# Depthwise convolution in two parts and row-by-row input split in the projection stage of a two-block hybrid model

## The reference

```python
def _grid_dwconv(u, w, grid_hw):
    b, t, ch = u.shape
    img = u.reshape(b, grid_hw[0], grid_hw[1], ch)
    out = lax.conv_general_dilated(img, w[:, :, None, :].astype(u.dtype), (1, 1), "SAME",
                                   dimension_numbers=("NHWC", "HWIO", "NHWC"),
                                   feature_group_count=ch)
    return out.reshape(b, t, ch)
```

## Time and profile before

| | us |
|---|---|
| three runs | 3732.07, 3729.84, 3727.48 |
| median | 3729.84 |
| the profiled execution, its time | 3728.76 |
| the profiled execution, its span | 3727.0 |
| PE busy in the span | 3390.9 |
| DVE busy | 1958.8 |
| ACT busy | 1435.2 |

### The profile page before, as it was taken

The page is one execution under the profiler, slowest core; times in us unless marked ns, Lnnn a source line. Parts: engine busy times, 40 slices in busy tenths (PEclk is TensorE's granted clock), DMA queues, the critical chain, the costliest instruction groups (busy, mean ns, idle before and its releaser), DMA issues.

```text
span 3727.0 us, 51106 instructions
## 1 busy us (share of the span) xinstructions
PE 3390.9 (91%) x20406; PEld 2828.4 (76%) x20406; DVE 1958.8 (53%) x2838; ACT 1435.2 (39%) x2196; POOL 218.7 (6%) x225
## 2 busy tenths in 40 slices
PE   1998776579999999999998999999999989999998
PEld 1776444457778877889855679999998557799998
DVE  6647577865534443446564544454446545444433
ACT  2532455344432333234345443343343444433322
POOL 1000033210000000000020000000000100000000
PEclk9999877569999999999999989999999989899999
DMA  5562101013333224223200002343432000023333
GB/s 194 182 201 93 51 15 59 10 55 113 108 118 117 90 94 164 94 88 121 81 1 29 24 24 83 106 140 92 136 113 76 1 29 24 30 86 109 113 94 100
DMA packets 94493, 321.82 MB, mean 86 GB/s; under 512 B 10352, under 2 KB 11632, under 8 KB 93488
## 3 DMA queue, kind: packets, MB, share of 16 engines
q1 hardware_dynamic: 76224, 249.66, 20.6%
q0 software_dynamic: 17312, 67.78, 5.2%
q10 hardware_dynamic: 720, 1.12, 0.1%
HBM read 295.38 MB, written 23.20 MB: 85 GB/s over the span
## 4 chain that ended last, share of the span: by engine, by line
PE 80%; DVE 12%; ACT 5%; DMA 1%; issue 1%; DVEq 0%; POOL 0%; ACTq 0%; SPq 0%; POOLq 0%
PE psum L146 76%; DVE mixer L171 4%; PE psum L149 3%; DVE mixer L181 2%; DVE wlo L171 1%; DVE arena L194 1%; DVE arena L171 1%; DVE junk L185 1%; ACT arena L155 1%; DVE mixer L198 1%; DVE region L171 1%; ACT whi L163 1%; ACT arena L163 0%; DMA stage<-in_wm 0%; ACT L155 0%
## 5 line engine op out<-in xcount | busy, mean ns | idle before, releaser
L146 PE MATMUL psum<-region,whi 128*128 128x260 f32 (+2 forms) x8896 | 1909.8, 312 | 22.8 <-DVE region L171 18.4
L146 PEld LDWEIGHTS psum<-region,whi 128*128 128x128 f32 (+1 forms) x8896 | 1444.1, 188 | 134.3 <-DVE region L171 16.8
L146 PE MATMUL psum<-region,wlo 128*128 128x260 f32 (+2 forms) x4448 | 1380.8, 310 | 0.0
L171 DVE TENSOR_TENSOR wlo<-stage,whi 128x1024 fp32r<-128x1024 f32 (+2 forms) x454 | 512.9, 1130 | 732.2 <-ACT whi L163 697.3
L146 PEld LDWEIGHTS psum<-region,wlo 128*128 128x128 f32 (+1 forms) x4448 | 839.7, 189 | 49.2
L163 ACT CAST whi<-stage 128x1024 fp32r<-128x1024 f32 (+2 forms) x454 | 441.7, 973 | 271.2 <-PE psum L146 177.7
L146 PE MATMUL psum<-arena 128*128 128x65 f32 (+8 forms) x2064 | 423.6, 356 | 2.8 <-ACT arena L155 1.2
L163 ACT COPY arena<-psum 128x512 f32<-128x512 f32 (+10 forms) x428 | 190.4, 445 | 416.3 <-PE psum L146 382.2
L146 PE MATMUL psum<-mixer 64*128 64x128 f32 (+6 forms) x1140 | 230.5, 446 | 121.0 <-DVE mixer L198 55.0
L146 PEld LDWEIGHTS psum<-arena 128*128 128x128 f32 (+4 forms) x2064 | 256.6, 181 | 100.3 <-issue 90.8
L154 ACT ACTIVATE arena<-psum 128x260 f32<-128x260 f32 (+1 forms) x236 | 101.0, 428 | 596.0 <-PE psum L146 595.6
(11 more groups left out here) (144 smaller groups left out, 2771.5 us busy)
## 6 DMA issues: line engine op xcount, KB each, us to landing
stage<-in_w SPq DMA_DIRECT2D x144, 512.0 KB, 3.5
stage<-in_wi SPq DMA_DIRECT2D x55, 512.0 KB, 4.2
stage<-in_wm SPq DMA_DIRECT2D x48, 512.0 KB, 3.4
stage<-in_wo SPq DMA_DIRECT2D x48, 512.0 KB, 3.5
stage<-in_wg SPq DMA_DIRECT2D x44, 512.0 KB, 3.3
stage<-in_wu SPq DMA_DIRECT2D x44, 512.0 KB, 3.3
stage<-in_wd SPq DMA_DIRECT2D x32, 512.0 KB, 3.3
arena<-xr_scratch POOLq DMA_DIRECT2D x7, 2080.0 KB, 8.8
```

The lines of the kernel that those rows point to most:

```text
L146: return Issued(self, self.e and self.e.matmul(out, w, x, start=start, stop=stop, skip_group_check=True))
L171: return Issued(self, e and e.tensor_tensor(out, a, b, op))
```

## The change

The convolution is cut in two by image rows. Part "a" makes output rows 0 to 6 (448 elements), which need image rows 0 to 7 only, and stands beside the half units of chunk 1 (ticks 11 to 22); its accumulators lie in a part of `vt` that chunk 2 fills later. Part "b" makes rows 7 to 15 (576 elements) in ticks 4 to 17 of chunk 2. The context's convolution moves to ticks 5 to 9 of chunk 1. The norm of chunk 1 starts at tick 2 of chunk 0 instead of tick 0. The wait on the whole chunk is gone: in the last half of a chunk, rows 2kk and 2kk+1 of the next chunk's input are split one tick after unit kk, when the product that used them has ended (`row_free`, `next_rows`). Six deferred rows move from chunk 1 to chunk 2.

```diff
-    CONV = [(m, part) for m in range(6) for part in range(3)] + [(m, 3) for m in range(5)]
+    ROWS_A, ROWS_B = (0, 7), (7, 16)
+    CONV_A = [(m, "a", part) for m in range(6) for part in range(3)]
+    CONV_B = [(m, "b", part) for m in range(6) for part in range(3)]
+    acc_a, acc_c = at(9000, 2, 448), at(9896, 2, 256)
 
     def proj_ticks(ch):
-        todo = [("norm", ch + 1, s) for s in NORM] if ch < 2 else [("conv", *c) for c in CONV]
-        heads = 6 if ch else 5
-        n = [0]
+        plan = [[] for n in range(11 + 12)]
+        if ch < 2:
+            for i, s in enumerate(NORM):
+                plan[i + (0 if ch else 2)].append(("norm", ch + 1, s))
+        if ch == 1:
+            for m in range(5):
+                plan[5 + m].append(("conv", m, "c", 0))
+            for i, c in enumerate(CONV_A):
+                plan[11 + i * 12 // len(CONV_A)].append(("conv", *c))
+        if ch == 2:
+            for i, c in enumerate(CONV_B):
+                plan[4 + i * 14 // len(CONV_B)].append(("conv", *c))
 
         def tick():
-            n[0] += 1
-            k = 1 if ch < 2 else 0 if n[0] <= heads else 2
-            out, todo[:k] = todo[:k], []
-            return out
-        return tick, todo
+            return plan.pop(0)
+        return tick
...
         if ch == 1:
-            return [19 + n] if n < 23 else []
-        return [42 + n] if n < 6 else []
+            return [19 + n] if n < 17 else []
+        return [36 + n] if n < 12 else []
...
+    def next_rows(ch, half, kk):
+
+        return (2 * kk, 2 * kk + 1) if ch < 2 and half == (2 if ch else 0) else ()
+
+    def row_free(ch, k):
+        return sproj.pe["unit", W.last["tok", ch - 1, 2 if ch > 1 else 0, k // 2]]
...
+        def act_row(ch, k):
+            N = chunks[ch][2]
+            if ch:
+                e.wait_ge(*row_free(ch, k))
+            e.wait_ge(*A["aff", ch, k])
+            e.copy(hh[:, k, 0:N], tmp[:, k, 0:N]).then_inc(*A.up("hi", ch, k))
         for ch, (src, s0, N, base) in enumerate(chunks):
-            tick, todo = proj_ticks(ch)
-            if ch:
-                e.wait_ge(*T["chunk", ch - 1])
-            for k in range(8):
-                e.wait_ge(*A["aff", ch, k])
-                e.copy(hh[:, k, 0:N], tmp[:, k, 0:N]).then_inc(*A.up("hi", ch, k))
+            tick = proj_ticks(ch)
+            for k in range(8 if ch == 0 else 0):
+                act_row(ch, k)
...
+                    for k in next_rows(ch, half, kk - 1) if kk else ():
+                        act_row(ch + 1, k)
+                for k in next_rows(ch, half, 3):
+                    act_row(ch + 1, k)
                 for t in range(N // 128):
                     ps = psum[:, bank.of["tok", ch, half, t], :]
...
                 for tap in range(part * 3, part * 3 + 3):
-                    v = img[:, tap // 3:tap // 3 + 16, tap % 3:tap % 3 + 64]
+                    v = img[:, r0 + tap // 3:r1 + tap // 3, tap % 3:tap % 3 + 64]
                     wc = P["convw"][:, m * 9 + tap:m * 9 + tap + 1]
                     if tap == 0:
-                        e.wait_ge(*A[("wi", 2, m), 0])
-                        e.wait_ge(*A["hi", 2, 7])
+                        e.wait_ge(*A[("wi", 1 if kind == "a" else 2, m), 0])
+                        if kind == "b":
+                            e.wait_ge(*A["hi", 2, 7])
```

More of the change, by code:

```diff
@@ L662, in dve_steps @@
             for m in (4, 5):
-                e.wait_ge(*sproj.act["conv", m])
+                e.wait_ge(*sproj.act["conv", m, "b"])
             e.wait_ge(*T["dt"])
@@ L815, in act_proj @@
                         ring += 1
-            for s in todo:
-                step(s)
         A.mark("end")
@@ L851, in step @@
                         e.scalar_tensor_tensor(acc, v, wc, acc, ALU.mult, ALU.add).then_inc(*D.up())
-                D.mark("conv", m, part)
+                D.mark("conv", m, kind, part)
                 return
@@ L876, in dve_proj, with dve_row @@
         dve_mod(e, beside)
-        for ch, (src, s0, N, base) in enumerate(chunks):
-            tick, todo = proj_ticks(ch)
-            if ch:
-                e.wait_ge(*T["chunk", ch - 1])
-            for k in range(8):
-                e.wait_ge(*A["hi", ch, k])
-                e.tensor_tensor(hl[:, k, 0:N], tmp[:, k, 0:N], hh[:, k, 0:N].bitcast(F32), ALU.subtract).then_inc(
-                    *D.up("lo", ch, k))
+        def dve_row(ch, k):
+            N = chunks[ch][2]
+            if ch:
+                e.wait_ge(*row_free(ch, k))
+            e.wait_ge(*A["hi", ch, k])
+            e.tensor_tensor(hl[:, k, 0:N], tmp[:, k, 0:N], hh[:, k, 0:N].bitcast(F32), ALU.subtract).then_inc(
+                *D.up("lo", ch, k))
+        for ch, (src, s0, N, base) in enumerate(chunks):
+            tick = proj_ticks(ch)
+            for k in range(8 if ch == 0 else 0):
+                dve_row(ch, k)
             for key in proj_gemms(ch):
@@ L894, in dve_proj @@
                     if (ch, half) == (2, 2):
-                        assert not todo
                         dve_steps(e, kk)
-            for s in todo:
-                step(s)
+                    for k in next_rows(ch, half, kk - 1) if kk else ():
+                        dve_row(ch + 1, k)
+                for k in next_rows(ch, half, 3):
+                    dve_row(ch + 1, k)
         D.mark("end")
```

44 lines of the change are left out of this document (23 added, 21 removed).

## The result

| | before | changed |
|---|---|---|
| median of 7 runs, us | 3729.84 | 3715.43 |
| lowest to highest | 3726.88 to 3732.21 | 3712.53 to 3719.31 |
| ratio, 95% interval | | 0.9963 [0.9952, 0.9975] |
| the profiled execution, its time | 3728.76 | 3715.06 |
| its span | 3727.0 | 3713.3 |

The change makes the kernel 14.4 us faster. The forecast was 33 us (3697), with 3690 to 3710 as its own range: the sign was right, the size wrong by more than half. The wide range reached to 3716 and just holds the result.

The account below looks back on a forecast made before the run. TensorE bounds the kernel (91% busy), but VectorE bounds chunk 2 with the convolution. Terms -28 - 6 + 7 - 6 = -33 us against 3728.76 give 3695.8, median 1.1 above: 3697 us, own range 3690 to 3710.

Parts of the forecast that it names:

- The wide range: Whole kernel: 3680 to 3716 us, taking in the bounds, the all-hidden case and half of the Silu rival.
- 1. Chunk 2's convolution work: Chunk 2 keeps nine rows of 64; 6 us of waits stand for the 34: -28 us, bounds -33 and -20.
- 2. The boundary between chunks 1 and 2: Rows split early, so the 4.25 us idle and slow first unit (1.5) go: -6 us, bounds -6 and -3.
- 3. Chunk 1 carries the other half: Chunk 1's steps 11 to 22 and context steps make units late: +7 us, bounds 2 and 16.
- 4. The boundary between chunks 0 and 1: Later norm and earlier rows mostly remove 2.82 us idle and 2.8 of the first unit: -6, bounds 0 and -10.
- 5. Extra taps: VectorE: 108 instructions for 54 on the same elements, 12.5 us more work, already counted in parts 1 and 3.
- the line: Tap time on VectorE interpolated between 0.50 us (256 elements) and 1.31 (1024): 0.70 on 448, 0.84 on 576.
- Every Silu costs its round: Rival: all 17 Silus leave VectorE idle 1.9 us on the path, 32 us come back: 3716 us, chance 0.14.
- All hidden: Rival: chunks 1 and 2 run at 5.60 us a unit, chunk 0 gives 10: 3680 us, chance 0.08.
- A tap does not get cheaper: Rival: row-strided taps on fewer rows keep 1.31 us, so 11 us slower: 3741 us, chance 0.05.
- Nothing arrives: Rival: the stage behind the projection is held by something fixed in time: 3730 us, chance 0.05.
- The signs named for it: Chunk 2 in about 137 us, idle start under 0.5, chunk 1 some 4 longer net of its quicker first unit.

Follow-up runs that it names:

- run 1: Changed kernel with part "a" of the convolution left out (54 taps, six Silus; output incomplete): 3697.76 us, ratio 0.9913.
- run 4: Changed kernel with the last third of part "a" moved from chunk 1 to chunk 2's first steps: 3707.05 us, ratio 0.994.
- run 7: Changed kernel with mostly one convolution part a step, 11 parts of "a" in chunk 1 and 7 in chunk 2 from step 0: 3698.43 us, ratio 0.9927.
- Run 9: Against run 7: 13 parts of "a" in chunk 1, two in steps 20 and 21, and chunk 2's table ending at step 17: 3700.94 us, ratio 0.9946.
- Run 3: Changed kernel's row split, with the convolution in one part in chunk 2 and norm and deferred rows as before the change: 3718.42 us, ratio 0.9974.
- run 6: Changed kernel with the load of chunk 2's x after chunk 1's first unit and chunk 2's norm two steps later: 3719.43 us, ratio 0.998.
- run 8: The edits of run 6 and run 7 together, on the changed kernel: 3705.43 us, ratio 0.9942.
- run 10: Run 9 nearly, with chunk 2's x loaded after chunk 1's first unit, its norm from step 5, context taps in steps 0 to 4: 3692.24 us, ratio 0.992.
- run 2: Changed kernel with the row-by-row split undone at both chunk boundaries, the convolution still in two parts: 3727.65 us, ratio 0.9991.
- run 5: Changed kernel with the split rows ahead of the convolution taps within each step of the last half: 3715.0 us, ratio 0.9971.
- run 11: The changed kernel once more, unaltered, for a second profile: 3717.55 us, ratio 0.9969.
- run 12: The kernel before the change once more, unaltered, for a second profile: 3728.62 us, ratio 0.9996.

## Why the prediction was wrong in size

By its own parts:

*1. Chunk 2's convolution work: right, 3.8 short.* Forecast -28.7 from unit 2.2 on, measured -24.86. The late units were to be 7 by 1.2 and 9 by 3.4; they are late by 1.45 and 3.80. The 0.7 for unit 12 did not come. What the sum left out is the restart: the products after unit 9's wait start every 0.43 us for the first half of the unit in place of every 0.23, and the unit took 8.08 (338.55 to 346.63), 2.5 over 5.60. The first taps were also dearer (below). The mechanism held: two thirds and more of the old waits are gone, and VectorE is no longer the bound there.

*2. The boundary between chunks 1 and 2: the failed step.* It said "rows 0 to 5 go while TensorE still has the last units, and rows 6 and 7 are ready 2.8 us after chunk 1's end", -5.3 with unit 2's 0.7; measured +8.24. This one step is 13.5 of the 23.4 us that are missing at S. Only rows 0 and 1 were split in time; rows 4 to 7 came 16.4 us after chunk 1's end (284.68 - 268.27). Even its lower bound, "VectorE still in a conv part", left a gain of 3. Its error was to take VectorE's state at the boundary as level with TensorE, though the steps ahead of it were summed in part 3: those sums covered units one at a time, and not the point where ACT's Silu, four evacuations and their stores empty VectorE for 6.85 us and leave it two steps behind, with steps of 6.0 us to come that cannot catch up. Runs 1, 4 and 7 take the work out of the last steps in three ways, and in each the boundary costs two plain units (11.2 us). Run 9 leaves two parts there, but no Silu ahead of half 1's evacuations, and has 11.19 too. How the 14.2 us divide between ACT's list and the taps of the last four steps is argued from the rows; no run keeps these taps and takes only that Silu away. Run 3 shows that the forecast gain of this part hangs on the look-ahead as well: with deferred rows between the units the wait moves to the next unit.

*3. Chunk 1 carries the other half: right.* Forecast +7, measured +8.77. Unit 15 is 1.15 late (0.9), unit 16 4.06 (3.7); the restart after it (unit 16 took 7.23) is what was left out. The "1.1 late" unit 17 did not show as a wait. But the sentence that "the lead covers" the last steps was wrong for VectorE: the lead was TensorE's in prepared units, while the rows have none.

*4. The boundary between chunks 0 and 1: the term mis-sized.* Forecast -6, measured -1.71 (-3.4 in the second pair of executions). The root product waited 4.20 us, as forecast, and chunk 1's first product came 7.8 us earlier (118.48 against 126.26), but its first unit then took 14.49 us instead of 8.42. The transfer was named ("still competes with the weights") and not priced. The weight load at 114.03 took 9.95 us, and run 6, which moves the load of x out of its way, starts unit 1.1 another 6.1 us earlier.

*5. Extra taps: right.* The taps on 448 and 576 elements, grouped by shape, from 190 to 372 us of the changed kernel (busy, mean ns, idle before them):

```profile
L181 DVE SCALAR_TENSOR_TENSOR mixer<-mixer,par 128x448 f32<-128x448 f32 x48 | 32.9, 685 | 1.7
L181 DVE SCALAR_TENSOR_TENSOR mixer<-mixer,par 128x576 f32<-128x576 f32 x32 | 26.2, 819 | 1.1
...
L176 DVE TENSOR_SCALAR mixer<-mixer,par 128x448 f32<-128x448 f32 x6 | 4.1, 680 | 0.4
L176 DVE TENSOR_SCALAR mixer<-mixer,par 128x576 f32<-128x576 f32 x4 | 3.2, 812 | 0.5
```

685 and 819 ns in pitches of 0.71 and 0.84 are the 0.70 and 0.84 of the line. 48 more taps at 0.685 + 0.819 - 1.285 = 0.219 us are 10.5 us, and six more first taps at 0.68 + 0.81 - 0.75 = 0.74 are 4.4: 14.9, where VectorE's busy time rose by 14.3 and 12.5 were forecast. The part over the forecast is in the first taps: the sum had 0.49 and 0.56 for them, hand-over included.

**The rivals.** "Every Silu costs its round" gave 3716, and the result is 3715.4, but it is a coincidence: by it chunk 2 would have kept most of its waits, and it lost 24.86 us of them; the Silu that hurt is one, ahead of the evacuations. "All hidden" was off everywhere; even from unit 2.2 to S the gain was 24.86 us of the 34. "A tap does not get cheaper" fell with the 685 ns. "Nothing arrives" fell with S: what the projection stage gives arrives in full.

**The signs named for it.** Chunk 2 from first to last product takes 153 us (268.59 to 421.71), not 137. Idle time at its start is under 0.5 (0.16), as said, and the sign was badly chosen: the waits came inside that first unit. Waits at units 15 and 16 came, that of unit 16 for `wlo`; the profile names no releaser for unit 15's. Chunk 1 from its first product to its end is 14.8 us longer and not 4, because its first unit is not quicker but slower. The next stage was to start by 433.76 - 30 = 403.8; of the kernels that do all the work only run 9 did (402.95), and run 10 but for 0.3.

## What to carry to other kernels

Where a table sets work beside products, don't only sum each step's load: follow each in-order engine to the point where something new must be early, and ask what stands in front of it there; a stretch in which VectorE is half idle on average still delivered its last third two steps late. An evacuation that waits for a store, with a Silu ahead and a weight cast behind it, couples three engines: put no vector work in the steps just before it (run 7's table gave 17.7 us of S over the change). A transfer moved away from one customer comes late for what waits for it, unless that moves as well: on the same tables of steps, or nearly, moving the load alone cost 4.4 us of S (run 8 against run 7), and moving both 1.1 (run 10 against run 9).

## What the runs showed of the hardware that was not expected

**The first tap is half as fast an element on 7 or 9 rows as on 16.** A TENSOR_SCALAR on 16 rows of 64 takes 0.75 us, on 7 rows 0.68 and on 9 rows 0.81: 0.13 us for 128 elements between the last two, 1.03 ns each, while on 1024 the same rate would give 1.27. On the context's 256 elements in one run it takes 0.35, so from there to 1024 an element costs 0.52 ns. The Trainium skill (VectorE: DVE Perf Modes, What auto-detection actually checks) has a rule that may be behind this: two elements a cycle for one SBUF source if the outermost dimensions of source and destination are both even, or equal. The trace agrees in that 16 rows are fast. For 7 and 9 rows it agrees only if the destination, whose rows touch, counts as one run of 448 or 576; counted as 7 or 9 rows it would be equal to the source. Neither that nor an even split (6 and 10 rows) was tried, so the cause is not shown.

**A wait costs more than its length.** After 3.80 us idle the unit at 338.55 took 8.08 us instead of 5.60, and unit 16 of chunk 1 7.23 after 4.06 us. The price is not fixed: unit 2.9 took 8.36 us in the second execution of the changed kernel and 7.22 or 7.23 in runs 1, 2, 5 and 6, each time after the same pause. The stretch 272 to 284 us had a granted clock of 0.65, and that from 325 to 342 0.85, between the two levels of 1.2 and 2.4 GHz.

**Identical code differs between executions by the granted clock.** The same products, much later in the program. Kernel before, stretch and one group of products:

```profile
3110.00:3130.00 20.00, 18.47 (x112) 12.00 (x112) 6.40 (x19) 8.04 (x17) 0.94 (x1) 0.74 0.30 107
```

```profile
3122.28 3.78 PE L146 MATMUL psum<-arena 96*128 96x512 f32 x4
```

The changed kernel at the same place:

```profile
3100.00:3120.00 20.00, 18.25 (x138) 12.33 (x137) 9.59 (x24) 9.21 (x19) 0.94 (x1) 1.00 0.31 107
```

```profile
3111.48 1.98 PE L146 MATMUL psum<-arena 96*128 96x512 f32 x4
```

3.78 us against 1.98 for the same four products, at 0.74 and 1.00. This place holds about 3.9 of the 4.1 us by which the two profiled executions differ behind the projection stage. In the second executions (runs 11 and 12) both kernels have 0.83 there, so the clock at this place comes with the execution: a gain of a few us must be read at the stage's end, and not from the span.
